# Two more projections of a two-block model in three rounded products, their low weight halves made by GpSimd, and the modulation pieces issued by SyncE

## The reference, cut to what matters

```python
mod = (c_act @ ada_w[layer] + ada_b[layer])              # 1024 -> 6144: shift, scale, gate, twice
h = _rmsnorm(x, norm_g[layer, 0]) * (1.0 + scale_m) + shift_m
# layer 0 mixer ("w_in"): proj = h @ w_in, 1024 -> 3072
#   a_val * sigmoid(a_gate) -> depthwise convolution of 31 taps -> layernorm -> silu
#   q, k (rotary), v, g     -> retention over 4 heads -> head norm, * silu(g)
#   mix = concat(a, r) @ w_out
x = x + gate_m * mix
h = _rmsnorm(x, norm_g[layer, 1]) * (1.0 + scale_f) + shift_f
x = x + gate_f * (jnp.square(jax.nn.relu(h @ w_fc1[layer])) @ w_fc2[layer])   # 1024 -> 4096 -> 1024
# layer 1 mixer: S5 (64 groups, complex diagonal states, both directions), GELU, GLU with w_glu_a, w_glu_b
```

## Time and profile before

| | before |
|---|---|
| median of 3 runs | 1256.76 us (1253.15 to 1258.34) |
| the profiled execution | 1256.46 us, span 1254.6 us |
| mean granted TensorE clock | 0.967 of 2.4 GHz |
| TensorE matmul busy | 1174.4 us (94%) |
| TensorE weight load busy | 1040.6 us (83%) |
| VectorE busy | 792.2 us (63%) |
| ScalarE busy | 547.5 us (44%) |
| GpSimd busy | 44.6 us (4%) |
| moved by DMA | 245.39 MB, 196 GB/s on average |

### The profile page before, as it was taken

How to read it: one execution, slowest core, us unless ns; L and a number is a source line. 1 busy time by engine, 2 the same in 40 slices (tenths; PEclk the granted TensorE clock), 3 DMA queues, 4 the chain that set the end, 5 groups by cost and what they waited for, 6 DMA issues and landing times.

```text
span 1254.6 us, 21837 instructions
## 1 busy us (share of the span) xinstructions
PE 1174.4 (94%) x9390; PEld 1040.6 (83%) x9390; DVE 792.2 (63%) x1342; ACT 547.5 (44%) x856; POOL 44.6 (4%) x71
## 2 busy tenths in 40 slices
PE   5999789999999998869999999999999999988798
PEld 2778568999888885469999999899888998877698
DVE  0178437788678765945666544688889636487635
ACT  1111223544210136444555433655677635466644
POOL 0100000000000000000000000000000000140000
PEclk8899979999999998989999999989999999998899
DMA  9977536889968844975445555234322453232141
GB/s 385 380 274 267 205 135 234 308 304 340 366 222 270 293 179 170 273 252 181 153 170 191 179 182 188 98 108 165 135 101 101 150 186 136 92 110 82 54 168 34
DMA packets 37344, 245.39 MB, mean 196 GB/s; under 512 B 4352, under 2 KB 5536, under 8 KB 8576
## 3 DMA queue, kind: packets, MB, share of 16 engines
q1 hardware_dynamic: 28128, 181.32, 41.9%
q0 software_dynamic: 6240, 43.94, 9.3%
q10 hardware_dynamic: 2880, 18.74, 3.6%
HBM read 224.19 MB, written 19.79 MB: 194 GB/s over the span
## 4 chain that ended last, share of the span: by engine, by line
PE 85%; DVE 5%; DMA 4%; ACT 4%; issue 1%; SPq 0%; DVEq 0%
PE ps L1297 18%; PE ps L1290 15%; PE ps L1292 14%; PE ps L1294 14%; PE ps L1375 3%; PE ps L1418 2%; DMA more<-in_ada_w 2%; PE ps L1318 2%; DMA ring<-in_blocks 2%; PE ps L1348 1%; PE ps L1708 1%; PE ps L1408 1%; PE ps L1811 1%; PE ps L1516 1%; PE ps L1359 1%
## 5 line engine op out<-in xcount | busy, mean ns | idle before, releaser
L1290 PE MATMUL ps<-sq_rounded,w_high_rounded 128*128 128x256 f32 x1120 | 323.5, 289 | 1.9 <-DVE ring_rounded L1938 1.0
L1294 PE MATMUL ps<-sq_rounded,ring_rounded 128*128 128x256 f32 x1120 | 318.8, 285 | 0.0
L1938 DVE TENSOR_TENSOR ring_rounded<-ring,w_high_rounded 128x1024 fp32r<-128x1024 f32 x208 | 246.6, 1227 | 98.4 <-ACT w_high_rounded L763 98.3
L1292 PE MATMUL ps<-hT_rounded,w_high_rounded 128*128 128x256 f32 x992 | 282.6, 285 | 0.0
L763 ACT ACTIVATE w_high_rounded<-ring 128x1024 fp32r<-128x1024 f32 x208 | 208.0, 1049 | 113.6 <-PE ps L1294 94.6
L1290 PEld LDWEIGHTS ps<-sq_rounded,w_high_rounded 128*128 128x128 f32 x1120 | 217.3, 194 | 10.9 <-issue 7.9
L1294 PEld LDWEIGHTS ps<-sq_rounded,ring_rounded 128*128 128x128 f32 x1120 | 217.1, 194 | 0.0
L1292 PEld LDWEIGHTS ps<-hT_rounded,w_high_rounded 128*128 128x128 f32 x992 | 192.5, 194 | 0.1
L1290 PE MATMUL ps<-more_rounded,w_high_rounded 128*128 128x256 f32 x448 | 128.2, 286 | 0.8 <-issue 0.8
L1294 PE MATMUL ps<-more_rounded,ring_rounded 128*128 128x256 f32 x448 | 127.5, 285 | 0.0
L1297 PE MATMUL ps<-big,ring 128*128 128x256 f32 x512 | 113.6, 381 | 0.0
(11 more groups left out here) (380 smaller groups left out, 1710.5 us busy)
## 6 DMA issues: line engine op xcount, KB each, us to landing
ring<-in_blocks SPq DMA_DIRECT2D x140, 1024.0 KB, 4.9
ada_w<-in_ada_w POOLq DMA_DIRECT2D x27, 1024.0 KB, 7.3
ada_more<-in_ada_w POOLq DMA_DIRECT2D x13, 1024.0 KB, 7.7
we_dram<-we_t ACTq DMA_DIRECT2D x8, 1024.0 KB, 7.6
ca_dram<-more ACTq DMA_DIRECT2D x8, 1024.0 KB, 11.4
ring<-we_dram SPq DMA_DIRECT2D x8, 1024.0 KB, 5.0
ring<-ca_dram SPq DMA_DIRECT2D x8, 1024.0 KB, 10.2
big<-in_ada_w SPq DMA_DIRECT2D x4, 1024.0 KB, 10.8
```

Source lines behind the costliest of these rows:

```text
L1290: nc.tensor.matmul(out, high[:, k, columns], x_high, start=start, stop=False, skip_group_check=True)
L1292: nc.tensor.matmul(out, high[:, k, columns], x_low, start=False, stop=False, skip_group_check=True)
L1294: last = nc.tensor.matmul(out, low[:, k, columns], x_high, start=False, stop=stop, skip_group_check=True)
L1938: nc.vector.tensor_tensor(rounded(w), w, w_high[:, c % 2, ks], ALU.subtract)\
```

## The change

Seven edits that hang together:

1. `w_in` and `fc2_0` join the split phases. Their high halves are rounded by ScalarE as in the others; the low halves are made by GpSimd (`lower_block`, two subtractions of 128 x 1024 a block), but for the first block of `w_in`, which VectorE lowers.
2. The activation of `w_in` is split: high into `sq` (ScalarE, with the shift), low into `hT` (VectorE). Block 0 of `w_in` is swept in three passes; blocks 8 and 9 have a split form of `project_tokens`.
3. The hidden activation of `fc2_0` is rounded by ScalarE (`round_hidden`, 16 of 128 x 512, into both halves of `ada_w`, `sq` and `hT`) and lowered by GpSimd (`lower_hidden`, 16 of 128 x 512).
4. `fc2_0` runs with the depth outside and the columns inside: all four quarters of its output stay open in PSUM (the fourth in the spare bank) and end with the last four blocks. VectorE's four residual steps all stand behind the rotations.
5. The 40 pieces are issued by SyncE, each behind the load of a block. `w_in` takes 17 pieces instead of 12, the retention 3 instead of 4, `fc2_0` only the closing step of the last group. From piece 40 on two slots are used.
6. The near kernels have four buffers (three in `big`, one in `w_high`), and the last two are loaded before `s5_out` blocks 1 and 2 are.
7. `h_rows` moves from `big` to `more`, and waits for the S5 stores; the rotations wait for eight blocks of `fc2_0`.

```diff
+ADA_AT = {"w_in": (1, 1, 2, 1, 2, 1, 2, 1, 2, 1, 2, 1), "retention": (3,), "w_out": (1, 1, 1, 1), "fc1_0": (1,) * 16,
+          "fc2_0": (1,)}
...
-    phase("fc2_0", [("fc2_0", k, n) for n in range(4) for k in range(4)])
+    phase("fc2_0", [("fc2_0", k, n) for k in range(4) for n in range(4)])
...
-SPLIT_LO = {"fc1_0": "vector", "glu": "vector", "fc1_1": "vector", "fc2_1": "vector", "xbc": "vector", "z": "vector",
+SPLIT_LO = {"w_in": "pool", "fc1_0": "vector", "fc2_0": "pool", "glu": "vector", "fc1_1": "vector", "fc2_1": "vector", "xbc": "vector", "z": "vector",
...
+LOWERED_FIRST = 1
...
-    NEAR_AT = (first_block["fc2_0"] + 10, first_block["fc2_0"] + 11, first_block["s5_out"] + 1 + RING,
-               first_block["s5_out"] + 3 + RING)
+    NEAR_AT = (first_block["fc2_0"] + 11, first_block["fc2_0"] + 15, first_block["s5_out"] + 1,
+               first_block["s5_out"] + 2)
...
-        s5_near = w_high_plain[:, :, :, :].rearrange("p s a b -> p s (a b)").rearrange("p s (q x) -> p s q x", q=4)
+        s5_near = [x.rearrange("p (q x) -> p q x", q=4)
+                   for x in (big[:, 2048:4096], big[:, 4096:6144], big[:, 6144:8192],
+                             w_high_plain[:, 1].rearrange("p a b -> p (a b)"))]
...
+        hid0_high = (ada_w[:, 0], ada_w[:, 1], sq, hT)
...
                 sp.dma_start(ring[:, b % RING].rearrange("p a b -> p (a b)"), dram["blocks"][laid_out[b]])\
                     .then_inc(w_here[b % RING], 16)
+                for n in piece_loads.get(b, ()):
+                    slot = ada_slot[n]
+                    turn = slot_users[slot].index(n)
+                    if turn:
+                        sp.wait_ge(ada_parts, slot_users[slot][turn - 1] - PIECES + 1)
+                    sp.dma_start(ada_slots[slot].rearrange("p a b -> p (a b)"), dram["ada_w"][n])\
+                        .then_inc(ada_here[slot], 16)
...
-            for n in range(PIECES, ADA_PIECES):
-                turn, slot = divmod(n - PIECES, ADA_SLOTS)
-                if turn:
-                    pool.wait_ge(ada_parts, n - PIECES - ADA_SLOTS + 1)
-                pool.dma_start(ada_slots[slot].rearrange("p a b -> p (a b)"), dram["ada_w"][n]).then_inc(ada_here[slot], 16)
...
+            def lower_hidden(u):
+
+                if u == 0:
+                    pool.wait_ge(a_low, SET_BASE["fc2_0"])
+                pool.wait_ge(a_high, SET_BASE["fc2_0"] + u + 1)
+                a, high = hid[:, 2 * u:2 * u + 2], hid0_high[u // 4][:, 2 * (u % 4):2 * (u % 4) + 2]
+                nc.gpsimd.tensor_tensor(rounded(a), a, rounded(high), ALU.subtract).then_inc(a_low, 1)
+
+            def lower_block(b):
+
+                c = split_place[b]
+                for half in range(2):
+                    pool.wait_ge(w_high_ready, 2 * c + half + 1)
+                    ks = slice(4 * half, 4 * half + 4)
+                    w = ring[:, b % RING, ks]
+                    nc.gpsimd.tensor_tensor(rounded(w), w, w_high[:, c % 2, ks], ALU.subtract).then_inc(w_low_pool, 1)
+
+            for n in range(LOWERED_FIRST, 12):
+                lower_block(first_block["w_in"] + n)
+            for u in range(4):
+                lower_hidden(u)
+
+            for j in range(16):
+                lower_block(first_block["fc2_0"] + j)
+                for u in {1: (4, 5), 2: (6, 7), 4: (8, 9), 5: (10, 11), 8: (12, 13), 9: (14, 15)}.get(j, ()):
+                    lower_hidden(u)
...
-            shift(0, 0, SHIFT_M)
+            round_to(first_block["w_in"] + 1)
+            for k in range(DT):
+                act.wait_ge(hn_ready, k + 1)
+                round_tiles(sq[:, k], hT[:, k], mod(0, SHIFT_M, k))
...
+            for j in range(16):
+                round_to(first_block["fc2_0"] + min(j + 2, 16))
...
+                if 16 + j in S5_TURN_AT:
+                    m = S5_TURN_AT.index(16 + j)
+                    copy_weights(m, (0, 1, 2, 3))
+                    store_weights(m)
+                if 15 + j in S5_TURN_AT and j > 0:
+                    m = S5_TURN_AT.index(15 + j)
+                    store_kernels(m - 1)
+                    store_outputs(m)
...
+            lower_to(first_block["w_in"] + LOWERED_FIRST)
+            for k in range(DT):
+                dve.wait_ge(a_high, SET_BASE["w_in"] + k + 1)
+                nc.vector.scalar_tensor_tensor(out=rounded(hT[:, k]), in0=hT[:, k], scalar=mod(0, SHIFT_M, k),
+                                               in1=rounded(sq[:, k]), op0=ALU.add, op1=ALU.subtract).then_inc(a_low, 1)
...
-                if m in (4, 6):
-                    residual("fc2_0", gate_f, m // 2 - 2, m // 2 - 1)
-            residual("fc2_0", gate_f, 2, 3)
...
+            dve.wait_ge(blocks_done, first_block["fc2_0"] + 8)
...
-            residual("fc2_0", gate_f, 3, 4)
+            residual("fc2_0", gate_f)
```

More of the change, by code:

```diff
@@ L79, with pieces_at @@
 ADA_SLOTS = 3
+LAST_OF_THREE = 40
 COPIES = 32
 ADA_GROUPS = ADA_PIECES // PIECES
+ADA_AT = {"w_in": (1, 1, 2, 1, 2, 1, 2, 1, 2, 1, 2, 1), "retention": (3,), "w_out": (1, 1, 1, 1), "fc1_0": (1,) * 16,
+          "fc2_0": (1,)}
+def pieces_at(phase, n=0):
+    first = PIECES
+    for name, counts in ADA_AT.items():
+        if name == phase:
+            first += sum(counts[:n])
+            return range(first, first + counts[n])
+        first += sum(counts)
+    raise KeyError(phase)
 def shape_constants():
@@ L205, in split_plan @@
             order.append(b)
-            counts[SPLIT_LO[name]] += 1
-            low[b] = counts[SPLIT_LO[name]]
+            engine = "vector" if b < LOWERED_FIRST else SPLIT_LO[name]
+            counts[engine] += 1
+            low[b] = (engine, counts[engine])
     return order, place, low
@@ L378, in program @@
         k_stored = sem("k_stored")
-        near_here = [sem(f"near_here{i}") for i in range(2)]
+        near_here = [sem(f"near_here{i}") for i in range(4)]
         rot_args = sem("rot_args")
@@ L505, in program @@
         ada_slots = (ada_w[:, 0], ada_w[:, 1], ada_more[:, 0])
+        ada_slot = {n: (n - PIECES) % ADA_SLOTS if n < LAST_OF_THREE else 1 + (n + 1) % 2
+                    for n in range(PIECES, ADA_PIECES)}
+        slot_users = [[n for n in ada_slot if ada_slot[n] == slot] for slot in range(ADA_SLOTS)]
+        behind_block = {n: first_block[name] + i for name in ("w_in", "w_out", "fc1_0")
+                        for i in range(len(ADA_AT[name])) for n in pieces_at(name, i)}
+        behind_block.update({n: first_block["w_in"] + 11 for n in pieces_at("retention")})
+        piece_loads = {}
+        for n in range(PIECES, ADA_PIECES):
+            turn = slot_users[ada_slot[n]].index(n)
+            b = behind_block[slot_users[ada_slot[n]][turn - 1]] + RING if turn else n - PIECES
+            piece_loads.setdefault(b, []).append(n)
         ada_rows, at = carve(ada_sum_flat, 2048, 1, NB)
@@ L617, in program @@
         units("fc2_0", 4, [(x_ready, 4 + n + 1) for n in range(4)])
+        for n in range(4):
+            ready[first_unit["fc2_0"] + n] = first_block["fc2_0"] + 12 + n + 1
         units("s5_in", 1, [(s5_e, n + 1) for n in range(8)])
@@ L885, in _ @@
             nc.scalar.activation(s5_dt, s5_logdt, ACT.Exp).then_inc(s5_fun, 1)
-            for n in range(20, 24):
+            for n in pieces_at("retention"):
                 modulation_row(n)
@@ L950, in _ @@
                     copy_weights(turn, (0, 1))
-                modulation_row(28 + n)
+                for piece in pieces_at("fc1_0", n):
+                    modulation_row(piece)
                 if turn is not None:
@@ L1314, in project_tokens @@
                 ps = pair(start_unit(phase, n))
+                if len(lhs) == 2:
+                    b = first_block[phase] + n
+                    engine, place = split_low[b]
+                    high, low = w_high[:, split_place[b] % 2], rounded(ring[:, b % RING])
+                    x_high, x_low = (rounded(x[:, :, :]) for x in lhs)
+                    for i in range(TT):
+                        for k in range(KB):
+                            if i == 0 and k % 4 == 0:
+                                pe.wait_ge({"vector": w_low_vector, "pool": w_low_pool}[engine], 2 * place - 1 + k // 4)
+                            at = slice(P * i, P * i + P)
+                            nc.tensor.matmul(ps[:, i], x_high[:, k, at], high[:, k], start=(k == 0), stop=False,
+                                             skip_group_check=True)
+                            nc.tensor.matmul(ps[:, i], x_low[:, k, at], high[:, k], start=False, stop=False,
+                                             skip_group_check=True)
+                            last = nc.tensor.matmul(ps[:, i], x_high[:, k, at], low[:, k], start=False,
+                                                    stop=(k == KB - 1), skip_group_check=True)
+                    last.then_inc(blocks_done, 1)
+                    return
                 w = start_block(phase, n)
@@ L1555, in _ @@
```

(9 more changed lines are left out.)

137 lines of the change are left out of this document (88 added, 49 removed).

## The result

The changed kernel takes 1322.85 us (median of 4 runs, 1321.92 to 1329.76); the kernel before, beside it on the same chip, 1257.55 (1253.15 to 1260.97). By these medians it is 65 us slower. The ratio on record, which is not the quotient of these two medians, is 1.0554, 95% interval 1.0521 to 1.0586: 5.5% slower. The profiled execution has a span of 1321.2 us against 1254.6.

What follows compares the result with a forecast made beforehand. TensorE bounds the kernel, with VectorE one step off the critical path; mixer +12, fc2_0 +40, s5_out -7 and clock +2 make +47 on 1256.5 us: 1304 us. Forecast 1285 to 1325, 8-in-10 range 1250 to 1342.

Steps and rivals of the forecast that it cites:

- What bounds: Whole kernel: TensorE holds 85% of the chain, so a cheaper product is worth its full price wherever TensorE is fed.
- GpSimd holds VectorE, for the length of its instruction: Where both engines work: one stands while the other runs, so each GpSimd instruction is time a working VectorE loses.
- 2.0 us a half: In w_in and fc2_0: length taken for one GpSimd subtraction of 128 x 1024, half a block of weights.
- Mixer stage, +12: From w_in through the retention: GpSimd's lowerings delay VectorE's taps, decay starts at 153.7 instead of 136.5; net +12 us.
- the 4.9 us: Behind the retention: one piece less, -1.0 us, and the 3.86 us wait for the last piece's load gone.
- the clock, +2: Mainly in the retention: TensorE starts at its lower clock level after longer pauses, +2 us.
- `fc2_0`, +40: fc2_0 stage: VectorE's S5 work plus GpSimd's lowerings set the pace, 177.3 us against 137.5, +40 us.
- SyncE's part, 0: SyncE's queue: 40 piece loads and their waits between the block loads cost nothing, 0 us.
- `s5_out`, -7: s5_out: the 6.58 us near-kernel wait goes and the first glu block no longer queues behind those loads, -7 us.
- Sum: Whole kernel: 12 + 40 - 7 + 2 = +47 us on 1256.5 us, giving 1304 us.
- the first: Rival, w_in and fc2_0: GpSimd's subtraction runs beside VectorE and the ports cost nothing, 1228 us; chance 0.13.
- the third: Rival, w_in: only plain two-tensor instructions are blocked, the taps not; mixer -10 instead of +12, 1282 us; chance 0.08.

Runs made afterwards that it cites:

- e5: Changed kernel with GpSimd's instructions cut to 8 elements a row and all 120 later tap passes waiting on their direct predecessor: 1229.12 us, ratio 0.9785.
- e1: Changed kernel with every GpSimd instruction cut to 8 elements a row, its low halves left out, all waits kept: 1257.24 us, ratio 1.0003.
- e2: Changed kernel with GpSimd copying each tile onto itself, rounded (one operand), instead of subtracting: 1277.05 us, ratio 1.0160.
- e4: Changed kernel with the first tile's instruction of each tap in the first batch waiting on its direct predecessor, not the one four before: 1319.45 us, ratio 1.0508.
- e9: Kernel before with one edit: SyncE issues the modulation pieces behind the weight blocks, no product newly split: 1248.56 us, ratio 0.9935.
- e3: Changed kernel with the last two near-kernel loads issued two blocks later, behind s5_out's third and fourth block: 1322.64 us, ratio 1.0507.
- e11: Changed kernel with the edits of e3 and e4 together: 1313.07 us, ratio 1.0468.
- e10: Kernel before with SyncE's pieces, only w_in's first four blocks split, and four near-kernel buffers with the later loads: 1238.43 us, ratio 0.9871.

## Why the prediction came out as it did

*What bounds.* Right. A cheaper product is worth its price only where TensorE is fed: e5 shows what the change would give once nothing holds the low halves, 2.15% or 27 us, in a kernel that leaves the low halves out.

*GpSimd holds VectorE, for the length of its instruction.* Right, and the base of the whole forecast: without GpSimd's work the loss goes (e1, e5), with the one-operand instructions seven tenths of it go (e2). The term was 2.0 us a half, between the two scalings of the copy; it is 2.1 as VectorE's loss and 2.38 as GpSimd's time alone. The hidden tiles were put at 1.0: 1.3 alone, 0.9 to 1.1 of loss. The prediction's estimate from the Trainium skill (GPSIMD Engine Reference, 3.1 Elementwise), 2.25 us, is between the two; this case's 2.38 us alone is 6% above it. The prediction looked at pairs of whole tensors only; tap 0, which reads one, is held too (5.69 us instead of 1.43).

*Mixer stage, +12.* It came out at +19.5 at the start of `fc2_0`, and this is the first step that failed. The decay was forecast at 153.7 and started at 158.98. The sum assumed that the two engines always take turns. In the first batch they did not: one GpSimd instruction stood for 20.57 us, so TensorE came late, and VectorE waited twice for rotary pieces that TensorE had not delivered (1.67 and 4.95 us). The sum had no such waits. Its other terms hold: from the first tap at 67.92 (69 forecast) to the end of the last at 159.06 are 91.1 us, of which 56.7 are work, 6.6 these waits and 27.8 the hold of 14 halves (28 forecast). e4 puts the decay at 155.26, 1.6 us from the forecast, of which its own tighter wait costs 1.5. "Taps 20.67, should take about 35" was wrong for the same reason; in the second batch the hold was there (37.74 instead of 27.01).

Behind the decay, up to the layernorm's sums, nothing of the 4.9 us came back (19.6 us before and after): the retention runs after a wait of 11.6 us, its values products took 2.07, 1.91, 1.51 and 1.03 us at a granted clock of 0.71, against 1.03 to 1.13 us at 1.00. Just behind it 3.0 us did come back, mostly because there it was the kernel before whose clock had dropped behind its 3.86 us wait (sums of 3.51 and 3.14 us instead of 1.99 each, a first block of `w_out` of 9.47 instead of 8.83). The two together are what the forecast had put down for the clock, +2. The stall of the two adjacent pieces was 0.76 us, not 1.3.

*`fc2_0`, +40.* Measured +47.7. The S5 turns were right in kind and in size: TensorE waits for VectorE's outputs and weights, 34 us, and the last output ends 141.7 us behind the stage's first product (140 forecast). VectorE was busy 172.1 us instead of 101.6 in e1, 70.5 more for 30 halves and 12 hidden tiles; at 2.1 and 1.0 us that is 75, so all but a few of GpSimd's instructions met work of VectorE. The step that fell short is what stands behind the last output, 37.3 us in the sum and 43.7 in the profile. There the prediction let 7 of the 12 us of the last six halves fall under VectorE's wait for ScalarE (+5). They met work instead: VectorE's last kernel step took 2.83 us instead of 0.41, one pass of the rotation 3.31 instead of 1.23 and its three fused passes 13.14 instead of 6.94, while the 7.01 us of waiting for ScalarE remained whole.

*SyncE's part, 0.* No run shows a cost of it; but the pieces as a whole gave 8 us (e9), where the prediction's terms for them come to 2.6: +5.0 and +1.3 in `w_in`, -4.9 behind the retention, -4.0 in `fc2_0`. The rest is for the most part the granted clock of the table above (0.97 instead of 0.88 behind the retention).

*`s5_out`, -7.* Wrong in sign: from the last residual to ScalarE's table load in `glu` it took 88.3 us instead of 85.9, +2.4. The 6.58 us wait went, as said. The step looked at what SyncE issues behind those loads only for `glu` and not for the score chunks between them (8.5 us in this profile); where these leave first (e3, e11, e10) 2 to 6 us come back. A second thing was in no term: the norm's sums need the squares of all residuals, which now stand at the very end, and are through 4.3 us behind the last residual instead of 2.3.

*Sum.* +47 against +66.6 in the profile, 19.6 more: 7.5 from the mixer stage, 7.7 from `fc2_0`, 9.4 from `s5_out`, less the 2 us put down for the clock, which are within them, and less 3.1 us by which the rest of the kernel, where nothing was edited, was shorter in this execution. The forecast's mechanism and side held, and so did the price of a half. What was short were three other steps, all to the same side: GpSimd kept out, the halves behind the last S5 output, and the score chunks. That 1322.9 still lies in the 1285 to 1325 of the forecast owes something to luck, as that range was worked out from the hold alone. Of the rivals, e5 shows what the first would have given (1229), and the taps of e4 and of the change's second batch refute the third: they are held like any other pass.

## What to carry to other kernels

An engine that is idle in the profile is not free: before work is moved to GpSimd, look at what VectorE does in that very stretch, and count each GpSimd instruction as VectorE's time, where both work in SBUF (here 2.1 of its 2.38 us). Where VectorE has a long run of passes without a pause and GpSimd's result is waited for, ask also whether GpSimd gets in at all; a wait of one pass on its direct predecessor opened the way, at about 0.12 us each here. Put such work where VectorE waits anyway (here before the taps), and try alone the small edits that come with a large one: the pieces by SyncE and the four near buffers, with a small part of the split, took 1.3% off here, while the whole split of `w_in` and `fc2_0` cost 6% (1.0554 / 0.9935).

## What was not expected of the hardware

- A GpSimd instruction can be shut out by a run of VectorE's passes, whatever its length: 14 to 22 us for one of 0.20 us (e1), 20.57 us for one of 2.38 us (the change), and the run of taps ends undisturbed. In the first batch it was let in, in every profile that shows this, just before the first VectorE instruction that waits for its direct predecessor. At other times it comes in at once: in the change's second batch each half entered, in e1's and e2's one was kept out to the end (22.3 and 24.6 us). Which of the two happens was not settled: arrivals 0.10, 0.14 and 0.15 us into a tap came in, those at 0.02, 0.09 and 0.27 to 0.33 were kept out, but one at 0.03 us into the first tap came in too (e1). What was shown is that a tighter wait of the taps on their predecessor (e4, e5) lets each one in.
- Once in, the two engines alternate instruction by instruction, and VectorE's pass is longer by most of GpSimd's time alone: 3.3 us instead of 1.22, 2.1 of 2.38. Passes of VectorE that read one tensor are held as well: tap 0's four took 5.69 us instead of 1.43, a 128 x 2048 pass 3.31 instead of 1.23.
- A one-operand rounding copy of 128 x 1024 by GpSimd takes 1.02 us, a two-operand subtraction of that size 2.38.
